# A two-layer hybrid decoder on one core: the last gate projection moved behind the S5 outputs, the S5 inputs carried through DRAM

## The reference, cut to what matters

```python
z = x @ p['w_in'] + p['b_in']                      # 1024 -> 512 + 512 + 1024 + 1024
u_a, u_b, z_ga, z_gb = split(z)
out_a = pool_mixer(u_a)                            # windowed means, then w_pool
h = scan(lam_bar, b_bar @ u_b)                     # S5 state, complex, 64 per group of 16 channels
y = gelu(real(c @ h) + d_skip * u_b)
out_b = y * sigmoid(y @ w_glu + b_glu)
merged = sigmoid(z_ga) * (out_a @ w_proj_a) + sigmoid(z_gb) * (out_b @ w_proj_b)
x = layer_norm(ALPHA * x + merged @ w_out)
```

## Time and profile before

| | |
|---|---|
| median of 3 runs | 1657.83 us (1656.47 to 1660.37) |
| profiled execution, its own time | 1657.29 us |
| its span, first to last instruction | 1655.5 us |
| granted TensorE clock, mean over the span | 0.987 of full |
| PE busy | 1587.1 us (96%) |
| DVE busy | 1337.0 us (81%) |
| ACT busy | 978.2 us (59%) |
| POOL busy | 145.9 us (9%) |

### The profile page before, as it was taken

How to read it: one execution, slowest core, us unless ns; L and a number is a source line. 1 busy time by engine, 2 the same in 40 slices (tenths; PEclk the granted TensorE clock), 3 DMA queues, 4 the chain that set the end, 5 groups by cost and what they waited for, 6 DMA issues and landing times.

```text
span 1655.5 us, 25658 instructions
## 1 busy us (share of the span) xinstructions
PE 1587.1 (96%) x9518; PEld 1372.0 (83%) x9518; DVE 1337.0 (81%) x1459; ACT 978.2 (59%) x899; POOL 145.9 (9%) x244
## 2 busy tenths in 40 slices
PE   7999999999999998999999999999999999999992
PEld 6887999999999796888888888888888888888882
DVE  5845777676686577989989989989989889889885
ACT  1233454443454446777777777777777777777771
POOL 3712000000172001000000000000000000000002
PEclk9999999999999999999999999999999999999996
DMA  7553545546355247999999999999999999999990
GB/s 179 153 167 83 154 137 171 176 145 197 122 167 138 78 144 249 370 385 342 364 391 338 363 389 339 358 393 334 369 390 336 368 387 338 361 395 336 363 359 26
DMA packets 216144, 449.28 MB, mean 271 GB/s; under 512 B 25624, under 2 KB 31688, under 8 KB 216062
## 3 DMA queue, kind: packets, MB, share of 16 engines
q1 hardware_dynamic: 206046, 436.23, 74.7%
q0 software_dynamic: 7952, 10.13, 2.6%
q10 hardware_dynamic: 2080, 2.01, 0.4%
HBM read 442.30 MB, written 3.01 MB: 269 GB/s over the span
## 4 chain that ended last, share of the span: by engine, by line
PE 86%; DVE 6%; ACT 3%; issue 2%; DMA 1%; POOL 1%; SPq 0%; ACTq 0%; DVEq 0%; POOLq 0%
PE bank L1672 83%; PE bank L1675 2%; DVE piece_lo L1032 2%; ACT piece_hi L779 1%; DVE ssm L1032 1%; DMA r_all<-in_b_glu_dram 1%; DVE r_all L1032 0%; DVE wide L1434 0%; ACT ssm L818 0%; DVE scr L1032 0%; DMA piece<-in_w_proj_a_dram 0%; POOL ssm L751 0%; DVE r_all L1382 0%; DVE m_lo L1032 0%; DMA xrow<-token_rows,ssm 0%
## 5 line engine op out<-in xcount | busy, mean ns | idle before, releaser
L1032 DVE TENSOR_TENSOR w_lo<-weights,w_hi 128x2048 fp32r<-128x2048 f32 x337 | 766.4, 2288 | 86.7 <-ACT w_hi L971 83.7
L971 ACT ACTIVATE w_hi<-weights 128x2048 fp32r<-128x2048 f32 x337 | 646.8, 1920 | 195.9 <-PE bank L1672 186.4
L1672 PE MATMUL bank<-w_hi,xg_hi 128*128 128x512 f32 x896 | 355.6, 397 | 2.3 <-DVE xg_lo L1032 1.4
L1672 PE MATMUL bank<-w_hi,xg_lo 128*128 128x512 f32 x896 | 350.1, 391 | 0.0
L1672 PE MATMUL bank<-w_lo,xg_hi 128*128 128x512 f32 x896 | 349.1, 390 | 0.0
L779 ACT ACTIVATE piece_hi<-piece 128x1024 fp32r<-128x1024 f32 x126 | 129.6, 1055 | 124.5 <-PE bank L1672 89.8
L1032 DVE TENSOR_TENSOR piece_lo<-piece,piece_hi 128x1024 fp32r<-128x1024 f32 x126 | 150.5, 1221 | 61.9 <-ACT piece_hi L779 60.8
L1672 PEld LDWEIGHTS bank<-w_hi,xg_hi 128*128 128x128 f32 x896 | 168.3, 188 | 37.8 <-DVE w_lo L1032 2.5
L1672 PEld LDWEIGHTS bank<-w_hi,xg_lo 128*128 128x128 f32 x896 | 168.2, 188 | 36.3
L1672 PEld LDWEIGHTS bank<-w_lo,xg_hi 128*128 128x128 f32 x896 | 168.5, 188 | 33.2
L1672 PE MATMUL bank<-w_hi,hidT_hi 128*128 128x512 f32 x448 | 176.6, 394 | 0.0
(11 more groups left out here) (301 smaller groups left out, 2138.2 us busy)
## 6 DMA issues: line engine op xcount, KB each, us to landing
weights<-in_w_moe_gate_dram SPq DMA_DIRECT2D x113, 1024.0 KB, 7.1
weights<-in_w_moe_up_dram SPq DMA_DIRECT2D x112, 1024.0 KB, 7.4
weights<-in_w_moe_down_dram SPq DMA_DIRECT2D x112, 1024.0 KB, 7.1
piece<-in_w_in_dram SPq DMA_DIRECT2D x48, 512.0 KB, 4.0
piece<-in_w_ffn_gate_dram SPq DMA_DIRECT2D x22, 512.0 KB, 4.6
piece<-in_w_ffn_up_dram SPq DMA_DIRECT2D x22, 512.0 KB, 3.8
piece<-in_w_ffn_down_dram SPq DMA_DIRECT2D x22, 512.0 KB, 3.9
piece<-in_w_out_dram SPq DMA_DIRECT2D x16, 512.0 KB, 4.3
```

The costliest lines, as they stand in the source:

```text
L971: act.activation(w_hi[s % PAIRS][:, :], ring_slot[:, :], ACT.Copy).then_inc(w_hi_ready, 1)
L1032: return dve.tensor_tensor(out, a, b, op)
L1672: signals(pe.matmul(out, lhsT, rhs, start=start, stop=stop, skip_group_check=True), signal)
```

## The change

Four edits, the same in both layers:

1. Gate projection 3 (tiles 12 to 15) moves from before `mix` to behind the transposes of the S5 outputs, into the stretch in which DVE and ACT compute the gelu. Its four weight pieces move behind those of `pa` in the plan. The six filler matmuls go. ACT empties the four tiles after the high parts of the gelu's result and ahead of the `glu` tiles; the wait for `ucol_in` moves with them.
2. The `h0` transposes go between gate 0 and gate 1, the `rows` transposes between gate 1 and gate 2. `mix` is made in two matmuls for each tile, 256 and 8 columns.
3. GpSimd stores `uchan` to DRAM in 4 transfers and fills `ucol` from there in 9.
4. `s5_inputs` may take low parts in between only up to the limit of gate tile 4, before up to that of tile 8.

```diff
@@ weight_plan
-        for key, at in [(("ub", l), PW), (("ua", l), 0)] + [(("gate", l, n), PW + SW + 512 * n) for n in range(4)]:
+        for key, at in [(("ub", l), PW), (("ua", l), 0)] + [(("gate", l, n), PW + SW + 512 * n) for n in range(3)]:
             add_rows(key, win[:, at:at + 512], l > 0)
...
             add_rows(("pa", l, c), w["w_proj_a"][l][:, 512 * c:512 * c + 512])
+
+        add_rows(("gate", l, 3), win[:, PW + SW + 1536:], l > 0)
         add_rows(("glu", l), w["w_glu"][l])
@@ psum_plan
-        tiles += [(("gate", l, m), "a") for m in range(16)]
-        tiles += [(("h0", l, r), "a") for r in range(2)] + [(("rows", l, s), "a") for s in range(2)]
+        tiles += [(("gate", l, m), "a") for m in range(4)] + [(("h0", l, r), "a") for r in range(2)]
+        tiles += [(("gate", l, m), "a") for m in range(4, 8)] + [(("rows", l, s), "a") for s in range(2)]
+        tiles += [(("gate", l, m), "a") for m in range(8, 12)]
...
-        tiles += [(("glu", l, m), "a") for m in range(4)]
+        tiles += [(("gate", l, m), "a") for m in range(12, 16)] + [(("glu", l, m), "a") for m in range(4)]
@@ GpSimd, columns
-                wait_emptied(pool, ("ub", l, 3))
+                by_channel = channels_dram[l].rearrange("(m p) t -> p m t", p=P)
+                for m in range(4):
+                    wait_emptied(pool, ("ub", l, m))
+                    pool.dma_start(by_channel[:, m, :], uchan[:, m, :]).then_inc(channels_kept, 16)
...
+                pool.wait_ge(channels_kept, 16 * 4 * (l + 1))
+                src = channels_dram[l].rearrange("(g c) t -> c g t", c=GC)
                 for j in range(CHUNK):
-                    for e in range(P // GC):
-
-                        src, dst = uchan[GC * e:GC * e + GC], to[GC * j:GC * j + GC, :, e, :]
-                        n = UC if j == CHUNK - 1 else NCH
-                        pool.dma_start(dst[:, :, 0:n], src[:, :, NCH * j:NCH * j + n]).then_inc(ucol_in, 16)
...
+                    to = ucol[GC * j:GC * j + GC]
+                    n = UC if j == CHUNK - 1 else NCH
+                    pool.dma_start(to[:, :, 0:n], src[:, :, NCH * j:NCH * j + n]).then_inc(ucol_in, 16)
@@ ACT, mixer
...
+
+                act.wait_ge(ucol_in, 16 * N_COLUMNS * (l + 1))
+                for m in range(12, 16):
+                    gate(m)
@@ DVE, mixer
-                s5_inputs(l, ("gate", l, 8))
+                s5_inputs(l, ("gate", l, 4))
...
                 gelu(l)
+                weights_lo(split_limit["gate", l, 15])
...
+                weights_lo(split_limit["glu", l, 0])
@@ TensorE, mixer
-                for n in range(4):
-                    project(("gate", l, n), x)
+                project(("gate", l, 0), x)
                 for r in range(2):
                     turn_over(claim(("h0", l, r))[:, 0:P], h0n[:, r, :], P, filled)
+                project(("gate", l, 1), x)
...
+                project(("gate", l, 2), x)
...
-                    mm(claim(("mix", l, g))[:, 0:T], wt[:, g, :], poolT[:, g, :], True, True, sig)
+                    ps = claim(("mix", l, g))
+
+                    mm(ps[:, 0:SEQ], wt[:, g, :], poolT[:, g, 0:SEQ], True, True)
+                    mm(ps[:, SEQ:T], wt[:, g, :], poolT[:, g, SEQ:T], True, True,
+                       through(filled, whole_used) if g == 3 else filled)
...
-                keep_warm(("yt", l, 3), 6)
+                project(("gate", l, 3), x)
                 project(("glu", l), rows_of(ys_hi, ys_lo), lambda k: pe.wait_ge(y_ready, 4 * l + k + 1))
```

More of the change, by code:

```diff
@@ L277, in trunk_kernel @@
                    + [(("down",), ("down", 1, NFT // 2 - 1))]
-                   + [(("gate", l), ("gate", l, 3, 3)) for l in range(DEPTH)]}
+                   + [(("gate", l), ("gate", l, 2, 3)) for l in range(DEPTH)]}
     per_pass = PassTiles()
@@ L482, in trunk_kernel @@
         vmat_ready, w1n_ready, bpair_zero, bpair_ready = map(sem, ("vmat_ready", "w1n_ready", "bpair_zero", "bpair_ready"))
-        kern_ready, toep_zero, toep_ready, ucol_zero, ucol_in, states_ready = map(
-            sem, ("kern_ready", "toep_zero", "toep_ready", "ucol_zero", "ucol_in", "states_ready"))
+        kern_ready, toep_zero, toep_ready, channels_kept, ucol_zero, ucol_in, states_ready = map(
+            sem, ("kern_ready", "toep_zero", "toep_ready", "s5_channels_stored", "ucol_zero", "ucol_in", "states_ready"))
         udec_ready, x_lo_ready, m_sum, m_hi_ready, h_hi_ready, h_lo_ready, bbar_ready = map(
@@ L834, in mixer, with gate @@
                         .then_inc(emptied["a"], 1)
-                for m in range(16):
-                    if m == 12:
-                        act.wait_ge(ucol_in, 16 * N_COLUMNS * (l + 1))
+                def gate(m):
                     act.activation(gates[:, m, :], trunk_tile(("gate", l, m))[:, 0:T], ACT.Tanh, scale=0.5,
                                    bias=colH[:, C_BIN + 24 * l + 8 + m:C_BIN + 24 * l + 9 + m]).then_inc(emptied["a"], 1)
+                for m in range(4):
+                    gate(m)
                 for r in range(2):
@@ L843, in mixer @@
                                    ACT.Copy).then_inc(emptied["a"], 1)
+                for m in range(4, 8):
+                    gate(m)
                 for s in range(2):
@@ L846, in mixer @@
                     act.activation(rows[s], tile_in(act, ("rows", l, s))[0:n, :], ACT.Copy).then_inc(emptied["a"], 1)
+                for m in range(8, 12):
+                    gate(m)
                 for g in range(4):
@@ L1812, in mixer @@
                 for g in range(4):
-                    sig = through(filled, whole_used) if g == 3 else filled
-                    mm(claim(("mix", l, g))[:, 0:T], wt[:, g, :], poolT[:, g, :], True, True, sig)
+                    ps = claim(("mix", l, g))
+                    mm(ps[:, 0:SEQ], wt[:, g, :], poolT[:, g, 0:SEQ], True, True)
+                    mm(ps[:, SEQ:T], wt[:, g, :], poolT[:, g, SEQ:T], True, True,
+                       through(filled, whole_used) if g == 3 else filled)
                 s5_matrices(l)
```

8 lines of the change are left out of this document (4 added, 4 removed).

## The result

The changed kernel takes 1649.76 us (median of 4 runs, 1648.94 to 1651.12) against 1658.94 for the kernel before in the same session (4 runs): ratio 0.9947, interval 0.993 to 0.9964. It is faster by 0.5%, and the forecast of 1657.5, range 1652 to 1663, missed it. The profiled execution has a span of 1648.0 us, before 1655.5.

The account below looks back on a forecast made before the run. TensorE, busy 96% of the span, was taken as the bound. Terms -8.56 + 2.8 + 2.9 + 1.2 + 1.6 = -0.1 us on 1657.29 gave 1657.2, stated as 1657.5 us for the median, range 1652 to 1663.

Parts of the forecast that it names:

- The S5 inputs through DRAM: Filling `ucol` by way of DRAM: done before TensorE reads it, ScalarE's wait long over, so 0.
- The hole: TensorE's gap during the gelu, ahead of `glu`: gate 3 fills it, -4.28 us in each layer, -8.56 in all.
- behind `glu` nothing was added: Second layer, from `glu` to the second `pb` tile: 0, at most +0.7 us.
- First layer behind `glu`: New TensorE wait for `pb`, whose second piece loads only after gate 3 ends: +2.8 us.
- The clock: TensorE's clock falls once, from the second layer's new wait: +1.6 us; first layer 0, up to 1.6.
- the rival "slower": The clock falls behind both new waits, and for longer: +5.1 us, 1662.5 us; chance 0.22.
- Second layer, gates: Longer TensorE waits in gates 1 and 2, for `pooling` and for low parts: +2.9 us.
- `mix` in two: Eight more matmul records of 8 columns in each layer's `mix`: +1.2 us for both layers.
- The rival "faster": The waits in both mixers stay small, no clock fall, `mix` costs nothing: -5.6 us, 1652 us; chance 0.28.

Follow-up runs that it names:

- a_spare126: The changed kernel with 126 GpSimd transfers of 512 bytes, DRAM to DRAM, added ahead of the second mixer: 1650.15 us, ratio 0.9949.
- a_late30: The changed kernel with 30 GpSimd transfers of 512 bytes, DRAM to DRAM, added behind those of the second mixer: last GpSimd drain 6.441 us, no total given.
- a_best: The changed kernel with `h0` and `rows` behind gate 2, `mix` in one matmul a tile, second-layer limit back at gate tile 8: 1643.49 us, ratio 0.9911.
- b_spare9: The kernel before with 9 GpSimd transfers of 512 bytes, DRAM to DRAM, added during the first layer's dense network: last GpSimd drain 8.809 us, no total given.
- b_gate3: The kernel before with only gate projection 3 moved behind the transposes of the S5 outputs: 1658.09 us, ratio 1.0001.
- a_lim8: The changed kernel with only the `s5_inputs` limit put back to gate tile 8 in both layers: 1662.24 us, one execution.

## Why the prediction was wrong

**The S5 inputs through DRAM: 0. This step failed.** It asked whether `ucol` is filled before TensorE reads it, and whether ScalarE waits for `ucol_in`; both answers were right. It gave the term as 0 without asking what the removed transfers cost on GpSimd itself. At the end of the program they cost something: GpSimd's last drain is on the path of the end, and for the 59 transfers fewer it is 4.73 us shorter, 80 ns each. Measured -4.7 us behind the last store, by edit 3 alone and by its undoing. The span was in the rows, the last store was not, and the 11.5 us between them would have asked the question. The sum with this term is -4.8, 1652.5 us: just inside the range, and still 2.7 above the measured median. The largest of the rest is 1.6 us of the clock in the second mixer, below.

**The hole, -4.28 in each layer: right.** In the second layer the section went from 10.51 to 17.77 with 11.77 us of gate 3 in it: -4.51, and behind `glu` nothing was added, as forecast. **First layer behind `glu`, +2.8: right.** The section went from 10.53 to 23.32, with 14.3 us of gate 3: hole and wait together -1.5, forecast -1.5. The chain is the one described: ScalarE gets `pb`'s second piece 5.3 us behind the end of gate 3 (forecast 4.9), and TensorE waits 2.85 us. The prediction sets a rule of the Trainium skill (DMA: Bandwidth & Descriptors, Anatomy of one DMA) beside the rows, 3.2 us for such a load; the section is about transfers that GpSimd issues, these are issued by SyncE, and the rows were nearer.

**The clock: counted too narrowly.** The forecast had one fall, behind the new wait of the second layer. The changed kernel's trace has one behind each new wait, 3.4 us each, as the rival "slower" said, but not the longer ones that it priced. In the first layer it cost little, as the forecast had allowed: from the last state transposes to the output projection the first mixer gave 1.3 us where the section up to `pb` gave 1.5. In the second layer the same wait of 3.15 us was followed by a fall in some executions and by none in others (a_spare126, a_late30), so it is a chance and no fixed term. And the old fall behind the chunk products was 3.4 us shorter, which gave 1.6 us back in "S5 outputs"; the forecast had nothing for that. The Trainium skill (TensorE: Matmul & The Clock Gate, Part 1) has the gate's window run freely, so that the number of slow matmuls changes; the lengths of 3.4, 6.8 and 10.2 us above agree with it. A fall is thus no term with a sign of its own.

**Second layer, gates, +2.9: right.** The section lost 43.23 - (50.61 - 11.77) = 4.4 us with the slow stretch in it, forecast 4.5. Taken apart, the fall is 1.3 us (forecast 1.6) and the gates 3.1, of which the low parts behind the table are 1.1, forecast 1.25.

**`mix` in two, +1.2: a little low.** 0.75 us a layer, 1.5 in all. In the first layer it may look as if the idle time in front of the chunk products had covered it, since that went from 0.92 to 0.26 us. It had not: with `mix` in one that idle time was 0.33 us in a_best and in b_spare9, so the 0.92 is one execution's, and a_best reaches its first chunk product 0.7 us sooner behind `pd` than the changed kernel.

**Edit 4 was not costed at all in the first layer.** The forecast took the changed order as a whole and so was spared the error, but a reader would take from it that moving gate 3 pays by itself. It doesn't (b_gate3, a_lim8): the limit has to move with the plan.

The rest, -0.8 us at the start, in the dense network and behind the second mixer, is of the size in which profiled executions of one kernel differ: the start alone was at 47.1 us in the changed kernel and at 49.0 in a_late30, with the same program up to there. The rival "faster" had the right sign at 0.28 and the wrong reason: no wait was smaller than forecast by more than 0.5 us.

## What to carry to other kernels

Look at the last microseconds of a span as at any other stretch: what stands between the last store and the end, and does it grow with something that the kernel does often? Here transfers issued by GpSimd from the second mixer on cost 80 to 82 ns each at the very end, though they held up neither mixer.

When an order of weights is changed, every limit that names a place in it changes its meaning, layer by layer: one such limit was worth 12 us in one layer and cost 1.1 in the other. Take a bundle of edits apart even when it is faster: here edit 2 stood in the way of the others.

Before the whole of a difference between two profiles is given to an edit, look where the clock was low in both. Runs that share the section and differ elsewhere (here a_spare126) show how much of it comes without the edit.

## What the runs showed of the hardware

The last drain of GpSimd lasts 3.995 us with 48 transfers from the second mixer on, 6.441 with 78 and 8.727 to 8.813 with 107. It repeats to the nanosecond where nothing in GpSimd's program differs, is blind to the kind and size of the transfers in these runs, and forgets those of the first mixer. The Trainium skill (DMA: Bandwidth & Descriptors, SWDGE vs HWDGE vs iDMA) says that descriptors of GpSimd's transfers are written by software; a cost for each transfer fits that, but no run here shows the mechanism.

TensorE's clock fell to 1.2 GHz behind the same small products for 3.4, 6.8 or 10.2 us, by which the next section moved by up to 3.6 us between kernels that do the same there. Behind one and the same wait of 3.15 us, in the same mixer program, it fell for 3.4 us in the changed kernel and not at all in a_spare126 and a_late30.
